# Two blocks of two layers with their passes written out, weight rings without skips, and the third group's weights converted behind the norm's root

## What is computed

```
for layer in 2:                                    # block 1
    h = rmsnorm(x); proj = h @ w_in                # XBC, QK, V, Z, GV, GU, GA, GB, GC
    y_a = spatial gating; y_b = state-space scan; y_c = differential attention
    x = x + (g0*(y_a @ w_a) + g1*(y_b @ w_b) + g2*(y_c @ w_c)) @ w_out       # BA, BB, BC, OUT
    h = rmsnorm(x); up = conv3(h @ w_up)           # UP: 22 groups
    x = x + (silu(gate) * val) @ w_down            # DN: 12 groups
for layer in 2:                                    # block 2
    h = rmsnorm(x); u,q,k,v,g = h @ w_in_2         # PU, Q, K, V, GP, GT
    x = x + (sig(g)*(pool(u) @ w_a) + sig(g)*(dilated attention @ w_b)) @ w_o # WP, WA, WB, OUT
    x = x + conv-gated FFN(rmsnorm(x))             # UP: 22 groups, DN: 12 groups
out = rmsnorm(x)
```

## Time and profile before

| | us |
|---|---|
| median of 3 runs (lowest, highest) | 1999.43 (1998.48, 2001.44) |
| the profiled execution: its time, its span | 2002.12, 2000.3 |
| PE busy in it | 1918.8 (96%) |
| POOL, DVE, ACT busy | 1182.1, 1061.0, 1044.5 |

### The profile page before, as it was taken

One profiled execution on the slowest core, in us unless ns is written; L12 is line 12 of the kernel. 1 busy time (PEld: TensorE's weight loads), 2 busy tenths in 40 slices (PEclk: granted clock), 3 DMA queues, 4 the chain that ended last, 5 costly groups with the idle time before them and its releaser, 6 DMA issues.

```text
span 2000.3 us, 36536 instructions
## 1 busy us (share of the span) xinstructions
PE 1918.8 (96%) x14342; PEld 1835.4 (92%) x14342; DVE 1061.0 (53%) x1421; ACT 1044.5 (52%) x1172; POOL 1182.1 (59%) x1094
## 2 busy tenths in 40 slices
PE   5999999999899999999999999999999999999998
PEld 5999998998799999899989999989988999989997
DVE  4657556765275655676634144455544233356553
ACT  5556634655364754465534356455444446455443
POOL 3555556766455655757755656456765565466665
PEclk9999999999999999999999999999999999999999
DMA  8887745555565563655664477455555557455554
GB/s 181 154 152 138 138 159 183 177 192 191 149 142 142 145 152 128 201 170 167 203 201 150 146 196 190 144 195 183 170 187 175 162 174 198 112 200 169 167 174 147
DMA packets 298971, 335.13 MB, mean 168 GB/s; under 512 B 8169, under 2 KB 266485, under 8 KB 298785
## 3 DMA queue, kind: packets, MB, share of 16 engines
q1 hardware_dynamic: 298664, 332.53, 58.6%
q10 hardware_dynamic: 120, 0.09, 0.0%
HBM read 331.52 MB, written 1.07 MB: 166 GB/s over the span
## 4 chain that ended last, share of the span: by engine, by line
POOL 53%; issue 39%; PE 6%; POOLq 0%; ACT 0%; DMA 0%; DVE 0%; DVEq 0%; SPq 0%; ACTq 0%
POOL w_low L350 53%; PE proj_ps L533 3%; PE proj_ps L544 1%; PE proj_ps L543 1%; PE proj_ps L545 1%; POOLq L348 0%; DMA x<-in_x 0%; ACT tmp L875 0%; PE chain_ps L600 0%; DVE x L1791 0%; ACT w_hi L361 0%; ACT L885 0%; ACT act_hi L885 0%; DVE x L1623 0%; DVEq L136 0%
## 5 line engine op out<-in xcount | busy, mean ns | idle before, releaser
L350 POOL TENSOR_TENSOR w_low<-w_raw,w_hi 128x256 fp32r<-128x256 f32 (+1 forms) x1088 | 1181.6, 1115 | 810.7 <-ACT w_hi L361 810.7
L533 PE MATMUL proj_ps<-act_hi,w_hi 128*128 128x256 f32 x3296 | 953.1, 289 | 49.8 <-POOL w_low L350 33.6
L533 PE MATMUL proj_ps<-act_lo,w_hi 128*128 128x256 f32 x3296 | 941.1, 286 | 0.0
L533 PE MATMUL proj_ps<-act_hi,w_low 128*128 128x256 f32 x3296 | 940.8, 285 | 0.0
L361 ACT ACTIVATE w_hi<-w_raw 128x2048 fp32r<-128x2048 f32 (+3 forms) x326 | 584.3, 1794 | 249.9 <-PE proj_ps L545 147.2
L533 PEld LDWEIGHTS proj_ps<-act_hi,w_hi 128*128 128x128 f32 x3296 | 640.7, 194 | 61.9 <-issue 49.3
L350 DVE TENSOR_TENSOR w_low<-w_raw,w_hi 128x1024 fp32r<-128x1024 f32 (+2 forms) x326 | 429.7, 1319 | 474.4 <-ACT w_hi L361 470.2
L533 PEld LDWEIGHTS proj_ps<-act_lo,w_hi 128*128 128x128 f32 x3296 | 641.0, 194 | 0.5
L533 PEld LDWEIGHTS proj_ps<-act_hi,w_low 128*128 128x128 f32 x3296 | 640.5, 194 | 0.0
L543 PE MATMUL proj_ps<-w_hi,act_hi 128*128 128x512 f32 x480 | 187.5, 391 | 0.0
L544 PE MATMUL proj_ps<-w_low,act_hi 128*128 128x512 f32 x480 | 186.9, 389 | 0.0
(11 more groups left out here) (219 smaller groups left out, 1418.9 us busy)
## 6 DMA issues: line engine op xcount, KB each, us to landing
w_raw<-in_w_in SPq DMA_DIRECT2D x126, 1024.0 KB, 7.7
w_raw<-in_ffn_w_up SPq DMA_DIRECT2D x44, 1024.0 KB, 5.2
w_raw<-in_w_up SPq DMA_DIRECT2D x44, 1024.0 KB, 5.1
w_raw<-in_ffn_w_down SPq DMA_DIRECT2D x16, 1024.0 KB, 5.1
w_raw<-in_w_down SPq DMA_DIRECT2D x16, 1024.0 KB, 5.0
w_raw<-in_w_branch_b SPq DMA_DIRECT2D x8, 1024.0 KB, 5.1
w_raw<-in_w_out SPq DMA_DIRECT2D x8, 1024.0 KB, 5.0
w_raw<-in_w_a SPq DMA_DIRECT2D x8, 1024.0 KB, 6.2
```

Source lines behind the costliest of these rows:

```text
L350: last = eng.tensor_tensor(group_view(wlo, slot, g)[:, part, :], group_view(raw, slot, g)[:, part, :], group_view(whi, HIGH_AT[b][n], g)[: ...
L533: last = mm(o, held, moved, start=start and k == ks[0] and q == 0, stop=stop and k == ks[-1] and q == 2, skip_group_check=shared)
```

## The change

Four things change. (1) The loops on PE, ACT, DVE and POOL become Python loops: every pass is written out, and all waits are for constants. (2) Slots are the group's number in the whole program, modulo 5 and 3, without skips; every conversion stands three groups behind; the conversions that nobody used are gone. (3) UP2's conversion moves to where XBC2's and PU2's are: behind `norm_root` on ACT, behind the first two `normed` on DVE. (4) `mean_square` stands behind `xg_low` instead of ahead of it, and is two `tensor_scalar` of one column instead of one `tensor_tensor` of two.

```diff
-def ring(count, slots, skips):
...
-        LOW_AT[1], LOW_LAST[1] = ring(NG[1], LOW, skips(1, "UP5", "UP11", "UP17"))
-        LOW_AT[2], LOW_LAST[2] = ring(NG[2], LOW, [])
-        HIGH_AT[1], HIGH_LAST[1] = ring(NG[1], HIGH, skips(1, "UP8", "UP14"))
-        HIGH_AT[2], HIGH_LAST[2] = ring(NG[2], HIGH, skips(2, "UP11"))
+        GROUPS = [(b, i, n, g) for b, G in ((1, G1), (2, G2)) for i in range(LAYERS) for n, g in enumerate(G)]
+        def at_group(b, i, n):
+            return BASE[b] + i * NG[b] + n
+        LATE = [at_group(b, i, at_name[b][name]) for b, names in ((1, ("XBC2", "UP2")), (2, ("PU2", "UP2"))) for i in range(LAYERS) for name in names]
+        def splits(b, i, n):
+            q = at_group(b, i, n) + HIGH
+            return [q] if q < len(GROUPS) and q not in LATE else []
...
+        def high_part(act, q):
+            g = GROUPS[q][3]
+            act.wait_ge(w_loaded[q % LOW], 16 * (q // LOW + 1))
+            act.wait_ge(group_done, q - HIGH + 1 + LOW)
+            act.activation(group_view(whi, q % HIGH, g), group_view(raw, q % LOW, g), ACT.Copy).then_inc(w_hi, 1)
...
-            for n in range(AHEAD):
-                load(2, LAYERS - 1, NG[2] + n, weight_source(2, 0, G2[n]))
...
-            with pe.Fori(0, LAYERS) as i:
+            for i in range(LAYERS):
...
                         norm_root(1, i, 1)
+                        split_late(1, i, "UP2")
                         norm_high(1, i, 1, A_H2)
...
             def mean_square(b, i, which):
                 dve.wait_ge(step("sq"), half_count(b, i, which, 1) + 1)
-                TTo(rstd[:, :], ssq[:, 0:2], ssq[:, 2:4], ALU.add).then_inc(step("ms"), 1)
+                for tt in range(TT):
+                    last = V.tensor_scalar(rstd[:, tt:tt + 1], ssq[:, tt:tt + 1], ssq[:, 2 + tt:3 + tt], None, ALU.add)
+                last.then_inc(step("ms"), 1)
-            def norm(b, i, which, a0, G=None):
-                mean_square(b, i, which)
+            def norm(b, i, which, a0, late):
                 xg_low(b, i, which, 2)
                 xg_low(b, i, which, 3)
+                mean_square(b, i, which)
                 norm_rstd(layer(b, i) * 2 + (which + 1))
                 normed(b, which, 0)
                 normed(b, which, 1)
-                if G is not None:
-                    split_behind(b, i, -1, G)
+                low_part(V, at_group(b, i, at_name[b][late]), False)
```

More of the change, by code:

```diff
@@ L28 @@
 DN_K = (4, 4, 4, 4, 3, 3)
-def ring(count, slots, skips):
-    at, place, last = 0, [], []
-    user = {s: s - slots for s in range(slots)}
-    for n in range(count + 2):
-        assert n != count or at % slots == 0
-        at += n in skips
-        place.append(at % slots)
-        last.append(user[at % slots])
-        user[at % slots] = n
-        at += 1
-    return place, last
 def build_program(nc, t_in, out):
@@ L64, in build_program @@
     LOW, HIGH = 5, 3
-    AHEAD = 2
     SLOT = 2048
@@ L956, in _ @@
             x_squares(1, 0, 0, 1)
-            for n in range(AHEAD):
-                high_part(act, 1, 0, n, G1)
-            with act.Fori(0, LAYERS) as i:
+            for q in range(2):
+                high_part(act, q)
+            for i in range(LAYERS):
                 xg_high(1, i, 0, 2)
@@ L1352, in _ @@
             TTo(bias_row[:, 0:511], pC[0:12, 510::-1], qkv[0:12, 1024:1535][:, ::-1], ALU.add).then_inc(step("bias_row"), 1)
-            for n in range(AHEAD):
-                low_part(V, 1, 0, n, G1, False)
-            with dve.Fori(0, LAYERS) as i:
-                norm(1, i, 0, A_H, G1)
+            for q in range(2):
+                low_part(V, q, False)
+            for i in range(LAYERS):
+                norm(1, i, 0, A_H, "XBC2")
                 def dt_abs():
@@ L1684, in _ @@
                     if g["name"] == "UP0":
-                        norm(1, i, 1, A_H2)
+                        norm(1, i, 1, A_H2, "UP2")
                     if g["name"] in FIRST:
@@ L1702, in _ @@
                         up_stream(1, i, n, g, G1)
-            with dve.Fori(0, LAYERS) as i:
+            for i in range(LAYERS):
                 dve.wait_ge(step("par_in2"), i * 32 + 32)
-                norm(2, i, 0, A_H, G2)
+                norm(2, i, 0, A_H, "PU2")
                 def b2_max(u):
@@ L1762, in _ @@
                     if g["name"] == "UP0":
-                        norm(2, i, 1, A_H2)
+                        norm(2, i, 1, A_H2, "UP2")
                     if g["name"] in FIRST:
```

102 lines of the change are left out of this document (40 added, 62 removed).

## The result

The changed kernel takes **1983.9 us** (median of 4 runs, 1981.57 to 1984.38) against 1999.25 for the kernel before, run beside it (4 runs, 1998.48 to 2001.44): 15.4 us or 0.8% faster, ratio 0.9919, 95% interval 0.9902 to 0.9936. The forecast was 1974.5 in 1966 to 1982. The sign was right, the gain was 9.4 us too large, and the time lies outside the range. The profiled execution took 1983.78 us with a span of 1982.0, so profile against profile the gain is 18.3 us where 25.0 were forecast; that shortfall of 6.7 us can be looked for in the traces. The other 2.7 us are a matter of which executions were profiled: I took off the 0.13% by which the kernel before's profiled execution lay above its median, and the changed kernel's happens to lie at its own. One execution of a later run, the kernel before with another source of weights, took 3755.88 us and is left out of its ratio.

The account below looks back on a forecast made before the run. PE's stream of matmuls was taken as the bound. Terms 19.2 + 9.7 - 0.1 - 3.8 = 25.0 us less took the profiled 2002.12 to 1977.1; with the median 0.13% lower, 1974.5 us, range 1966 to 1982.

Parts of the forecast that it names:

- What bounds the kernel: PE's stream of matmuls, busy 1918.8 of 2000.3 us; its waits lie behind skips, at block 1's second pass and norm turns.
- Skips, 19.2 us: UP stage, six places behind skipped slots: stalls go and three groups take 17.28 us; 19.2 us less, bounds 17.7 to 19.2.
- The later sum: Norm turns: sum, root and reciprocal now follow xg_low; 0.6 us more at one PU turn, 0.5 less at the other.
- UP2 behind the root, 3.8 us more: Four UP turns: spread comes earlier, but UP3's conversion is late and PE waits for POOL; 3.8 us more in all.
- The rival of a cheap third group: UP turns: late conversion doesn't delay UP3 as POOL catches up; 3.6 us less instead of 3.8 more, 1967; 10%.
- Block 1's second pass, 9.7 us less: Turn from block 1's first pass: without the jump back XBC3 starts at 555.0 instead of 564.75; bounds 6.4 to 10.6.
- the second pass keeps part of its wait: Block 1's second pass: jump cheap, DVE and ACT late for another cause; only PE's 2.1 us comes back, 1982; 12%.
- The signs to look for: PE's w_low waits fall from 36.2 to about 25 us, UP7 to UP9 take 17.3, UP3 waits 1.1 to 1.3 for POOL.

Follow-up runs that it names:

- the second pair of traces: Both kernels profiled again with no edit: the changed kernel took 1982.26 us (6 runs), the kernel before 2003.16 us (one run).
- the combined version: Changed kernel with UP2 converted early, last addition to x first, and sum of squares ahead of the low parts as one operation: 1975.07 us, ratio 0.9875.

## Why the prediction was wrong where it was

**What bounds the kernel** was read rightly: nearly all that was won or lost lay at skips and turns, and PE's busy time stayed at 96%.

**Skips, 19.2 us.** Right. The starts of PE's groups in the two traces give 2.99 and 2.95 us in the first pass, 2.96 and 2.95 in the second, 2.88 and 4.38 in block 2: 19.1 us. Putting back the order alone costs 16.6 us at the same places. Of the other 2.5, 1.5 was the lower clock at the last place, and 0.16 us a place went with the loops: the kernel before written out takes 20.08 from UP7 to UP9 where it took 20.27 and 20.24.

**The later sum.** Right: 0.6 us more at the first PU turn, 0.5 less at the second. From the turn's transposes to the spread it is 4.5 us, forecast 4.36. That it is a loss at every turn once the jump is gone (22.9 instead of 22.2), the combined version shows.

**UP2 behind the root, 3.8 us more.** Right in size (3.6 between the traces, 3.7 when taken back) and in mechanism: UP3 waits 1.17 us for POOL. The rival of a cheap third group falls.

**Block 1's second pass, 9.7 us less.** This is the step that failed: 4.1 us came back. "Written out, this turn should look like the one from block 1 into block 2" took the PU turn's loads for granted, and they come from another tensor. With loads in time the turn does take 23.6 us, where I had 23.4. With XBC1's late load it takes 29.0, which is 5.6 too many: PE starts XBC0 5.03 us behind DN11 instead of 1.38, and takes 2.0 more to the spread at its lower clock. From the spread to XBC3 it is 14.64 us, as forecast.

The reading of the old stall was wrong too. I put all of it on the jump. With fast transfers the looped turn is only 2.1 us longer than the written-out one, and most of that is ACT's table loads. They stood in the trace between DVE's sum and the spread, and I didn't mention them. The other 7.4 of the 33.1 us came with w_in's transfers.

The whole shortfall of 6.7 us can be followed from group to group in the two traces. The turn gives 5.6. From XBC3's start to XBC5's it is 575.24 - 557.11 = 18.1 us where it was 16.7, at a granted clock of 0.81 instead of 0.90: 1.5 more. At the program's end it is 0.5 more. In block 2 it takes 0.45 and 1.94 us less from PU3 to OUT0 in the two passes, which I hadn't forecast; 1.5 of that is one group, WA3, at a clock of 1.00 instead of 0.77. And the first pass reaches UP0 1.55 us later. These add up to 6.75. All but the last come again in the second pair of traces. The first pass doesn't: there UP0 comes 1.56 us *sooner*, and XBC1's load, though late in the first pass as well (landed at 22.26, before at 20.56), isn't the cause, as XBC5 starts at 68.94 and 68.92. The difference arises at GA1, which took 7.57 and 8.79 us in the two traces of the kernel before and 8.90 and 6.64 in those of the changed one, at granted clocks of 0.79, 0.66, 0.65 and 1.00: chance of an execution.

I had the load's number in my hands and didn't price it: in the kernel before XBC1 landed at 518.15 + 9.12 = 527.27, and ACT began to copy it at 527.61, with 0.3 us to spare. A wait with so little margin is a term of the sum, with a bound above zero.

**The rival "the second pass keeps part of its wait"**, at 1982 and 12%, had the nearest number and the wrong cause: what stayed was a late load, not a late start of DVE and ACT. But it saw more than I credited. The jump is cheaper in itself than I read, 3.57 us on PE and 5.18 on DVE with fast transfers, against 7.09 and 11.16, and ACT did load tables there; those went with the loop as well, so they kept no part of the wait. The Trainium skill's 108 ns for a compare-and-branch ("Advanced Engine Details and Errata", Control Flow Timing) is near the 83 ns at the loop's exit, and far from all jumps back measured here: 7.09, 6.49 and 7.15 us with w_in, 3.38 to 3.64 otherwise.

**The signs to look for.** Waits for `w_low` fell from 36.2 to 16.9 us, further than the 25 that I gave, but part of them now stands under issue: written out, the same wait is named differently in the table (PU3's was 1.34 us for POOL, and is 1.19 marked issue). I would have done better to name groups and starts than a total by releaser.

**Shown and not shown.** Shown: that XBC1's late load is what is missing at the turn (two ways of making it land in time, the same 23.6); that the slow transfers go by the address in w_in; that the set of slow columns changes with PE's code and not with that of DVE, ACT and POOL; that PE's fetch at the jump begins 3 to 3.8 us later with w_in. Argued only: that it waits behind weights in the DMA engines; the loads' source changes both, and no run separates them. Open: by what rule PE's code moves w_in's slow columns.

## What to carry to other kernels

Before a stall is priced as gone, list what is due right behind it and by how much it was early; here a transfer with 0.3 us to spare took the stall's place. A duration in a busy stretch, of a jump or of a load, is not a constant of the operation: look for the same thing in a stretch with other transfers before carrying it over; here block 2's jump, in the same trace, took half as long. Look on every engine for what stands at the start of a loop; here two table loads on ACT went with it. And a change that writes out a program can alter which parts of an untouched tensor are read slowly, so compare load times tensor by tensor before explaining waits by the order of instructions.

## What the runs showed of the hardware that was not expected

- The same 1 MB load, 1024 pieces of 1 KB, holds the queue from 2.7 to 15.8 us by its first column. In w_in, with rows of 8208 numbers (32,832 bytes), the long times come every 1024 columns (4096 bytes), alike in every execution of a program, and mostly in both passes; the mean is 7.0 to 7.3 us. From w_in_2, with rows of 7680 numbers, the mean is 5.4 to 5.5 us, and the time from issue to landing 5.7 and 5.8 in the second pass.
- Writing out PE's loops moved the slow set from column remainders of about 768 by 1024 to about 256 and raised the mean from issue to landing from 9.8 to 12.5 us, with hardly a change in the mean time of holding the queue (7.0 and 7.2 us). Writing out the other engines' loops, 264 KB more of scratch in DRAM, or 32 or 128 more PE instructions moved nothing.
- A jump back to the loop's start cost PE's queue 7.09, 6.49 and 7.15 us beside transfers from w_in, and 3.38 to 3.64 us beside transfers from w_in_2 (five jumps). The fetch of 16 KB itself took 0.9 to 1.2 us; it began 4.0 to 4.8 us behind the branch in the first case and 1.0 in the second.
- ACT's loop of block 1 brought three table loads of 1.28 us (79 in the program, 76 written out), two of them on the path to the norm's factor at the second pass.
